# Hybrid decoder step on one core: a turn's first score block is copied out of PSUM before the last gate function and the table load of the turn before

## The chip, the cores and the metric

The kernel runs on one core of a Trainium2 chip. The metric is the device time of one execution in microseconds (us). A core has TensorE (PE; its weight loads are listed as PEld), VectorE (DVE), ScalarE (ACT), GpSimd (POOL) and SyncE (SP, here the only issuer of DMAs). Each engine works through its own instruction stream in order; the streams meet at semaphores.

## The reference, cut to what matters

One inference step of a one-layer decoder, for a prompt of 16 + 1024 positions and 8 running sequences with one new token each. Stick-breaking attention and an RG-LRU branch run beside each other, are merged by sigmoid gates, and a ConvFFN follows.

```python
z = jnp.einsum('bqhgd,bshd->bhgqs', qb, kp) * SB_SCALE + bias_f
log_keep = jnp.where(mask, jax.nn.log_sigmoid(-z), 0.0)      # softplus of z
w = jnp.where(mask, jnp.exp(jax.nn.log_sigmoid(z) + tail), 0.0)   # tail: sum of later log_keep
...
r = sigmoid(xb @ w_rgate + b_rgate); i = sigmoid(xb @ w_igate + b_igate)
a = jnp.exp(-RG_C * r * softplus(-lam))
u = jnp.sqrt(-jnp.expm1(2.0 * log_a)) * i * xc
h = scan(a, u); rnn = h * gelu(gr)
x = x + (gate_a * attn + gate_b * rnn) @ w_out
```

The kernel writes softplus(z) as max(z, 0) + ln(1 + exp(-|z|)), every sigmoid by a tanh, and the square root through exp and ln. So ScalarE needs two table sets in turn: one with the gelu and tanh, one with exp and ln.

## The kernel before, in words

Five phases follow each other: the first projections, the mixing phase (here from about 200 to 1090 us), the output projection, the FFN and the last norm. The change lies in the mixing phase (`phase_mix`).

The mixing phase has 8 turns (`i` from 0 to 7), one for each pair of heads and for one tile of 128 RNN channels; the loop is unrolled. A turn has 17 slots (`s`), one for each block of 64 queries, in the order of `BLOCK_ORDER`. All four engines have their order written out by hand, and each slot has work from several pipeline stages:

- TensorE, slot s: values of the block of slot s-4 (L1355), transposes of the weights of slot s-3 (L1336), a few pieces of the RNN and gate projections (L87), in slots 2 to 9 the decode scores (L1395, they need ScalarE's copy `k_t`) and in slots 1 to 8 transposes of a K page (L1407), then the scores of slot s+1 (L1315, the mask at L1322). Only in slot 0 are the scores of slot 0 made as well, last but one: after the page products of the turn before (L1378). The scores of slot s+1 wait for `z_copied` of slot s, since there is one PSUM tile for scores (`p_z`).
- ScalarE, slot s: `score_out` copies the scores out of PSUM twice, as |z + bias| (L1029) and as z + bias (L1030, this one gives `z_copied`); in slots 2 to 9 the copy `k_t` (L1067); the exponential of the weights of slot s-2 (L1054); the high part of the next projection tile (`high_part`, L1002, in slot 1 among others); softplus by an exp (L1084) and a ln (L1085); the projection chunks out of PSUM (L1049); and one part of the RNN tail of the turn before (`act_late`: an exp in slot 0, a ln in slot 1, a ln in slot 2, an exp in slot 5).
- VectorE, slot s: values out (L1137), max(z, 0) of slot s-1 (L1144), its running sum, which needs softplus (L1151), copies of the transposed weights (L1129), z minus the sum (L1157), in slot 1 among others the low part of the projection tile, which needs the high part (L1117), and parts of the RNN tail; the one in slot 1 (L728) gives the stage on which `act_late` waits in the same slot.

At the head of slot 0 of every turn but the first, ScalarE works off the gate functions of the turn before: a load of the gelu and tanh set, a gelu, four tanh (together `act_gates`, all at L678 by the helper `act_step`), a sixth function that waits for VectorE's `gated` (L711), and `act.preload_act_table_set` (L692), which loads the exp and ln set. All of them come ahead of `score_out` of slot 0.

Turns 2, 4 and 6 begin with a new group of K and V heads: SP loads K anew, and the scores of slot 0 wait for it. Turns 1, 3, 5 and 7 keep K. In all of them, TensorE waits at the end of the turn before for the last V pages (L1378).

Of the kernel before, what the change touches and what calls it, by code (L numbers as in the profile page):

```python
# [20 lines left out]
KT = D // P  # L21
# [32 lines left out]
def nth(turn, per_turn, index, credit=0):  # L54

    return turn * per_turn + (index + 1 + credit)
# [599 lines left out]
class Branch:  # L656
# [23 lines left out]
    def act_gates(self, act, i):  # L680

        _, ga = self.views(i)
        gr, gb, rg, ig, rc = self.gr, self.gb, self.rg, self.ig, self.rc
        self.act_step(act, i, gr[:, :], gr[:, :], ACT.Gelu_apprx_tanh)
        self.act_step(act, i, gb[:, :], gb[:, :], ACT.Tanh, scale=0.5)
        self.act_step(act, i, rg[:, :], rg[:, :], ACT.Tanh, bias=rc[:, 2:3], scale=0.5)
        self.act_step(act, i, ga, ga, ACT.Tanh, scale=0.5)
        self.act_step(act, i, ig[:, :], ig[:, :], ACT.Tanh, bias=rc[:, 3:4], scale=0.5)
        act.wait_ge(self.gated, nth(i, 1, 0))

        self.act_step(act, i, gr[:, :], rg[:, :], ACT.Tanh, T_R, bias=rc[:, 1:2], scale=rc[:, 1:2])
        act.preload_act_table_set("natural_log_exp_and_others")  # L692

# [107 lines left out]
def phase_mix(nc, g, branch, first_tiles, sem):  # L801
# [3 lines left out]
    with ctx:  # L805
# [79 lines left out]
        with nc.Block() as block:  # L885
# [108 lines left out]
            @block.scalar  # L994
            def _(act):
                own = Chain(act, act_step)
                act.sem_inc(proj_out, 2)

                def high_part(slot, chunks, turns):
                    act.wait_ge(w_in[slot], turns)  # L1000
                    act.wait_ge(proj_done, chunks)
                    act.activation(w_hi[:, slot, :, :], w_raw[:, slot, :, :], ACT.Copy).then_inc(w_hi_ready, 1)  # L1002

                act.wait_ge(inits, 2)
                for h in range(2):
                    rows = slice(HD * h, HD * (h + 1))
                    act.activation(never[rows, :], z[rows, QB * h:QB * (h + 1)], ACT.Copy).then_inc(masks, 1)
                act.activation(ident_b[:, :], g.ident[:, :], ACT.Copy).then_inc(masks, 1)
                act.sem_inc(z_copied, 1)
                high_part(0, CHUNK_NS, 16)  # L1010
                act.preload_act_table_set("natural_log_exp_and_others")

                def score_out(i, s, first):

                    b, q0, nq, nk = unit(s)
                    so, zs, pz = sums[:, soft_cols(s)], z[:, z_cols(s)], p_z[:, 0:min(nk, 1024)]
                    act.wait_ge(qk_done, nth(i, SLOTS, s, SLOTS))
                    if not first or s >= 2:
                        act.wait_ge(arg_ready, nth(i, SLOTS, s - 2, 1))
                    if not first or s > LAG:  # L1020
                        act.wait_ge(wt_turned, nth(i, GROUPS, group_of(s - LAG, 0) - 1, GROUPS))
                    if b == 16:
                        act.activation(so[:, 1024:nk], p_z_last, ACT.Abs, bias=bias[:, 0:1])
                        act.activation(zs[:, 1024:nk], p_z_last, ACT.Identity, bias=bias[:, 0:1])
                        so, zs = so[:, 0:1024], zs[:, 0:1024]
                    elif b >= 2:
                        pz = p_z[:, 0:1024].rearrange("p (a c) -> p a c", a=2)[:, :, 0:nk // 2]
                        so, zs = (x.rearrange("p (a c) -> p a c", a=2) for x in (so, zs))
                    own.mark(act.activation(so, pz, ACT.Abs, bias=bias[:, 0:1]))  # L1029
                    act.activation(zs, pz, ACT.Identity, bias=bias[:, 0:1]).then_inc(z_copied, 1)  # L1030

                def chunk_out(i, n, first):

                    what, c = CHUNK_ORDER[n]
                    cols = slice(CW * c, CW * (c + 1))
                    if what == "ga":
                        out = g.mix[:, bass.ds(i + 1, 1), cols].rearrange("p a c -> p (a c)")
                    else:
                        out = {"xr": xr, "gr": gr, "gb": gb, "rg": rg, "ig": ig}[what][:, cols]
                    if n == 0 and not first:  # L1040
                        act.wait_ge(xc_ready, nth(i, 1, 0) - 1)
                    if what in ("gr", "rg", "gb") and c == 0 and not first:
                        done = {"gr": S_ROOT, "rg": S_STATE}
                        if what in done:
                            act.wait_ge(branch.stage, nth(i - 1, STAGES, done[what]))
                        else:
                            act.wait_ge(branch.tail_done, nth(i, 1, 0) - 1)
                    act.wait_ge(proj_done, nth(i, CHUNK_NS, n, CHUNK_NS))
                    act.activation(out, p_proj[:, CHUNK_BANK[n], 0:CW], ACT.Copy).then_inc(proj_out, 1)  # L1049

                def weights(i, s):

                    act.wait_ge(arg_ready, nth(i, SLOTS, s, 1))
                    act.activation(z[:, z_cols(s)], z[:, z_cols(s)], ACT.Exp).then_inc(w_ready, 1)  # L1054

                def slots(i, first):
                    own.turn(0, i, 2 * SLOTS + 3)
                    own.step(act.activation(bias[:, 0:1], g.bias_pair[:, bass.ds(i, 1)], ACT.Copy))
                    for s in range(SLOTS):
                        if s == 0 and not first:  # L1060
                            weights(i, -2)
                            act.wait_ge(proj_out, nth(i, CHUNK_NS, -1, 2))
                            branch.act_gates(act, i - 1)
                        score_out(i, s, first)
                        if 2 <= s <= 9:
                            act.wait_ge(page_used, nth(i, 16, s - 2, 2))
                            act.activation(k_t[:, :, :].rearrange("p a c -> p (a c)"), p_kt[:, :],  # L1067
                                           ACT.Copy).then_inc(kt_out, 1)
                        if s >= 2 or s == 1 and not first:
                            weights(i, s - 2)  # L1070
                        if s in W_AT:
                            t = W_AT.index(s)
                            high_part((t + 1) % 2, nth(i, CHUNK_NS, CHUNK_NS - 1) if t == 0
                                      else nth(i, CHUNK_NS, TILE_LAST[t - 1], CHUNK_NS), 16 * (nth(i, 2, (0, 1, 1, 2)[t])))
                        if s == 11:
                            act.wait_ge(zd_read, nth(i, 1, 0))
                            own.step(act.activation(softd[:, :, :], zd[:, :, :], ACT.Abs))
                            own.step(act.activation(softd[:, :, :], softd[:, :, :], ACT.Exp, scale=-1.0))
                            act.activation(softd[:, :, :], softd[:, :, :], ACT.Ln, bias=1.0).then_inc(softd_done, 1)
                        for n in EARLY_OUT.get(s, ()):  # L1080
                            chunk_out(i, n, first)
                        so = sums[:, soft_cols(s)]
                        act.wait_ge(act_step, own.base + own.n)
                        own.step(act.activation(so, so, ACT.Exp, scale=-1.0))  # L1084
                        act.activation(so, so, ACT.Ln, bias=1.0).then_inc(soft_done, 1)  # L1085
                        for n in chunks_of(s):
                            if n not in EARLY_OUT.get(s, ()):
                                chunk_out(i, n, first)
                        if not first and s in ACT_LATE_AT:
                            branch.act_late(act, i - 1, ACT_LATE_AT[s])  # L1090
                        if s == 13:
                            act.wait_ge(argd_ready, nth(i, 1, 0))
                            act.activation(zd[:, :, :], zd[:, :, :], ACT.Exp).then_inc(wd_ready, 1)
                    assert own.n == 2 * SLOTS + 3

                for i in range(KT):
                    slots(i, i == 0)
                weights(KT, -2)
                weights(KT, -1)
                act.wait_ge(proj_out, nth(KT, CHUNK_NS, -1, 2))  # L1100
                branch.act_gates(act, KT - 1)

            @block.vector
            def _(dve):
# [1122 lines left out]
```

## Time and profile before

| | |
|---|---|
| median of 3 runs | 2044.91 us (2043.24 to 2045.83) |
| profiled execution | 2048.54 us, span of its records 2046.8 us |
| TensorE granted clock, mean | 0.965 of 2.4 GHz |
| TensorE busy | 1893.0 us, 92% of the span |
| VectorE busy | 1210.6 us, 59% |
| ScalarE busy | 928.8 us, 45% |
| one turn of the mixing phase, from one load of the gelu set to the next | 109 to 112 us |

The span runs from the first to the last recorded instruction; the execution has 1.7 us around it. A busy share is an average over five phases with different limits. For this change the stretch of some 20 us at the head of a turn is what is to be read, seven times: turn 1 begins near 300 us, turn 7 near 964 us.

### The profile page before, as it was taken

To read this page: it belongs to the slowest core of one execution; us is meant where nothing else is said; L and a number is where in the kernel's file an instruction comes from. 1 tells how busy PE (TensorE), PEld (TensorE's weight loads), DVE (VectorE), ACT (ScalarE), POOL (GpSimd) and SP (SyncE) were. 2 spreads that over 40 slices of the span, in tenths; PEclk is the share of its full clock that TensorE was granted. 3 is DMA by queue.
4 is the path that set the end of the run, shared out by engine and by line. 5 is a ranking of instruction groups with operands and counts; after the bars stand their busy time and mean duration, and the time that the engine had idled before them with its cause. 6 is when DMAs were issued, how large, how long until landed. Compare 5 with 4: busy or idle time off the path is not lost. (4 is left out here: it accounts for less than half of the span.)

```text
span 2046.8 us, 38456 instructions
## 1 busy us (share of the span) xinstructions
PE 1893.0 (92%) x14580; PEld 1730.1 (85%) x14580; DVE 1210.6 (59%) x1999; ACT 928.8 (45%) x1506; POOL 199.2 (10%) x98
## 2 busy tenths in 40 slices
PE   6998999989998999899996978999999999999985
PEld 5897878878787878687884768999999999999984
DVE  6101667768685858577776435665566556656655
ACT  5121677776867686777775221221222122212213
POOL 0121000000000000000000002221122112211210
PEclk9999999989998999999997989999999999999988
DMA  4334213141314232331313321111111111111104
GB/s 134 109 89 111 79 46 97 44 109 40 99 48 103 63 79 68 82 85 43 98 36 100 123 73 42 58 52 41 41 51 51 41 41 51 51 37 45 51 11 182
DMA packets 198685, 143.47 MB, mean 70 GB/s; under 512 B 58289, under 2 KB 187890, under 8 KB 198528
## 3 DMA queue, kind: packets, MB, share of 16 engines
q1 hardware_dynamic: 198554, 141.73, 24.4%
q8 instruction: 82, 1.34, 0.3%
q14 instruction: 49, 0.40, 0.1%
HBM read 124.31 MB, written 17.61 MB: 69 GB/s over the span
## 5 line engine op out<-in xcount | busy, mean ns | idle before, releaser
L87 PE MATMUL d_p_up<-n_hi,d_w_hi 128*128 128x346 f32 x1056 | 342.2, 324 | 16.3 <-ACT d_up L1824 8.3
L87 PE MATMUL d_p_up<-n_hi,d_w_lo 128*128 128x346 f32 x1056 | 341.4, 323 | 0.0
L87 PE MATMUL d_p_up<-n_lo,d_w_hi 128*128 128x346 f32 x1056 | 341.3, 323 | 0.0
L1927 DVE TENSOR_TENSOR mix<-mix,d_p_down 128x346 f32<-128x346 f32 x264 | 136.1, 515 | 268.2 <-PE d_p_down L1976 268.2
L87 PE MATMUL b_p_proj<-n_hi,b_w_hi 128*128 128x350 f32 x768 | 264.9, 345 | 16.0 <-DVE b_w_lo L1117 9.4
L1779 POOL TENSOR_TENSOR d_w_lo<-w_raw,d_w_hi 128x1024 fp32r<-128x1024 f32 x45 | 109.0, 2424 | 1468.6 <-ACT d_w_hi L1810 1468.6
L87 PE MATMUL b_p_proj<-n_lo,b_w_hi 128*128 128x350 f32 x768 | 251.7, 328 | 0.0
L87 PE MATMUL b_p_proj<-n_hi,b_w_lo 128*128 128x350 f32 x768 | 251.4, 327 | 0.0
L1824 ACT ACTIVATE d_up<-d_p_up 128x346 f32<-128x346 f32 x132 | 60.1, 457 | 401.8 <-PE d_p_up L87 401.8
L87 PEld LDWEIGHTS d_p_up<-n_hi,d_w_hi 128*128 128x128 f32 x1056 | 200.6, 190 | 17.4 <-ACT d_up L1824 9.1
L87 PEld LDWEIGHTS d_p_up<-n_lo,d_w_hi 128*128 128x128 f32 x1056 | 201.0, 190 | 0.0
L87 PEld LDWEIGHTS d_p_up<-n_hi,d_w_lo 128*128 128x128 f32 x1056 | 200.7, 190 | 0.0
L1151 DVE TENSOR_TENSOR_SCAN b_sums<-b_sums 128x720 f32<-128x720 f32 (+16 forms) x136 | 171.1, 1258 | 8.0 <-ACT b_sums L1085 3.4
L87 PEld LDWEIGHTS b_p_proj<-n_hi,b_w_hi 128*128 128x128 f32 x768 | 149.5, 195 | 18.4 <-issue 10.1
L1976 PE MATMUL d_p_down<-d_a_lo,d_wd_hi 128*128 128x346 f32 x480 | 153.8, 320 | 0.0
L1976 PE MATMUL d_p_down<-d_a_hi,d_wd_hi 128*128 128x346 f32 x480 | 153.8, 320 | 0.0
L1976 PE MATMUL d_p_down<-d_a_hi,d_wd_lo 128*128 128x346 f32 x480 | 153.7, 320 | 0.0
L1137 DVE COPY mix<-b_p_misc 128x64 f32<-128x64 f32 (+1 forms) x136 | 29.7, 219 | 205.6 <-PE b_p_misc L1355 205.3
L87 PEld LDWEIGHTS b_p_proj<-n_lo,b_w_hi 128*128 128x128 f32 x768 | 149.2, 194 | 0.0
L87 PEld LDWEIGHTS b_p_proj<-n_hi,b_w_lo 128*128 128x128 f32 x768 | 148.1, 193 | 0.0
L1029 ACT ACTIVATE b_sums<-b_p_z,b_bias 128x720 f32<-128x720 f32 (+16 forms) x136 | 94.8, 697 | 109.9 <-PE b_p_z L1322 97.6
L1315 PE MATMUL b_p_z<-b_k_in,b_q_in 64*64 64x360 f32 (+16 forms) x1024 | 96.5, 438 | 20.4 <-issue 20.4
(262 smaller groups left out, 3837.8 us busy)
## 6 DMA issues: line engine op xcount, KB each, us to landing
w_raw<-in_w_in SPq DMA_DIRECT2D x45, 512.0 KB, 4.6
w_raw<-in_w_up SPq DMA_DIRECT2D x45, 512.0 KB, 3.9
b_page<-in_cache_k SPq DMA_DIRECT2D x128, 128.0 KB, 2.1
b_page<-in_cache_v SPq DMA_DIRECT2D x128, 128.0 KB, 2.1
w_raw<-in_w_down SPq DMA_DIRECT2D x22, 512.0 KB, 3.5
b_q_in<-q_scr SPq DMA_DIRECT2D x272, 32.0 KB, 2.2
mix<-in_x_prompt SPq DMA_DIRECT2D x8, 512.0 KB, 7.1
w_raw<-in_w_out SPq DMA_DIRECT2D x8, 512.0 KB, 3.5
```

Of the source, the lines that this page charges most:

```text
L87: last = pe.matmul(out, w[:, k, :], x[:, k, col:col + width], start=(k == 0 and w is w_hi and x is x_hi), stop=(k == KT - 1 and w is w_lo))
L1029: own.mark(act.activation(so, pz, ACT.Abs, bias=bias[:, 0:1]))
L1137: dve.tensor_copy(g.mix[:, bass.ds(i if s >= 0 else i - 1, 1), FIRST + q0:FIRST + q0 + nq] .rearrange("p a c -> p (a c)"), p_av[:, 0:nq]). ...
L1151: dve.tensor_tensor_scan(pos[:, ::-1], so[:, ::-1], pos[:, ::-1], 0.0, ALU.add, ALU.add)\
L1315: last = pe.matmul(banks[bank][QB * a:QB * (a + 1), 0:k1 - k0], q_in[rows, Q_AT[s], a, :], k_in[rows, k0:k1], start=True, stop=k1 <= diagonal)
L1779: pool.tensor_tensor(w_lo[:, slot, :, :], w_raw[:, raw, :, :], w_hi[:, slot, :, :].bitcast(F32), ALU.subtract).then_inc(lo_ready, 1)
L1824: act.activation(up[:, u % 2, F0 + FW * c:F0 + FW * (c + 1)], p_up[:, n % 2, 0:FW], ACT.Copy).then_inc(up_out, 1)
L1927: dve.tensor_tensor(to, to, p_down[:, n % 4, 0:FW], ALU.add).then_inc(down_out, 1)
L1976: last = pe.matmul(p_down[:, n % 4, 0:FW], w[:, k, P * tile:P * (tile + 1)], a[:, k, F0 + FW * c:F0 + FW * (c + 1)], start=(k == 0 and w i ...
```

## The change

The sixth gate function and the table load leave `act_gates` and become a method of their own. In turns 1 to 7, ScalarE now runs them behind `score_out` of slot 0 instead of ahead of it. At the end of the phase, where no scores follow, both methods are called one after the other. No instruction is added or removed, no semaphore and no buffer is changed.

```diff
@@ class Branch
         self.act_step(act, i, ig[:, :], ig[:, :], ACT.Tanh, bias=rc[:, 3:4], scale=0.5)
+
+    def act_last_gate(self, act, i):
+
+        gr, rg, rc = self.gr, self.rg, self.rc
         act.wait_ge(self.gated, nth(i, 1, 0))
-
         self.act_step(act, i, gr[:, :], rg[:, :], ACT.Tanh, T_R, bias=rc[:, 1:2], scale=rc[:, 1:2])
         act.preload_act_table_set("natural_log_exp_and_others")
@@ phase_mix, ScalarE, slots(i, first)
                             branch.act_gates(act, i - 1)
                         score_out(i, s, first)
+                        if s == 0 and not first:
+                            branch.act_last_gate(act, i - 1)
                         if 2 <= s <= 9:
@@ phase_mix, ScalarE, after the last turn
                 branch.act_gates(act, KT - 1)
+                branch.act_last_gate(act, KT - 1)
```

## Rows read from the trace of the kernel before

**Rows 1.** The page, busy time and share of the span by engine.

```profile
PE 1893.0 (92%) x14580; PEld 1730.1 (85%) x14580; DVE 1210.6 (59%) x1999; ACT 928.8 (45%) x1506; POOL 199.2 (10%) x98
```

**Rows 2.** Timeline, ScalarE, head of turn 1 (start us, us, instruction, idle before).

```profile
300.52 1.28 ACT L678 ACT_TABLE_LOAD   x1
301.82 1.08 ACT L678 ACTIVATE r_gr<-r_gr 128x1050 f32<-128x1050 f32 x1
...
306.86 1.25 ACT L678 ACTIVATE r_gr<-r_rg,r_rc 128x1050 f32<-128x1050 f32 x1
308.13 1.28 ACT L692 ACT_TABLE_LOAD   x1
309.43 0.86 ACT L1029 ACTIVATE b_sums<-b_p_z,b_bias 128x720 f32<-128x720 f32 x1
310.18 0.85 ACT L1030 ACTIVATE b_z<-b_p_z,b_bias 128x720 f32<-128x720 f32 x1
310.93 0.80 ACT L1084 ACTIVATE b_sums<-b_sums 128x720 f32<-128x720 f32 x1
311.76 0.80 ACT L1085 ACTIVATE b_sums<-b_sums 128x720 f32<-128x720 f32 x1
```

**Rows 3.** Timeline, TensorE, turn 1: scores of slots 0 and 1.

```profile
308.13 0.20 PE L1322 MATMUL b_p_z<-b_never,b_ident_b 64*64 64x64 bf16 x2
311.14 0.37 PE L1315 MATMUL b_p_z<-b_k_in,b_q_in 64*64 64x168 f32 x4 [2.81 <-issue]
```

**Rows 4.** Timeline, TensorE, scores of slot 1 in turns 3, 5 and 7.

```profile
531.62 0.84 PE L1315 MATMUL b_p_z<-b_k_in,b_q_in 64*64 64x168 f32 x8 [3.17 <-issue]
...
753.38 0.84 PE L1315 MATMUL b_p_z<-b_k_in,b_q_in 64*64 64x168 f32 x8 [3.42 <-issue]
...
975.12 0.84 PE L1315 MATMUL b_p_z<-b_k_in,b_q_in 64*64 64x168 f32 x8 [3.91 <-issue]
```

**Rows 5.** Timeline, VectorE and ScalarE, slots 1 and 2 of turn 1.

```profile
314.06 1.66 DVE L1151 TENSOR_TENSOR_SCAN b_sums<-b_sums 128x720 f32<-128x720 f32 x1
...
314.90 1.05 ACT L1002 ACTIVATE b_w_hi<-w_raw 128x1024 fp32r<-128x1024 f32 x1
...
317.36 1.22 DVE L1117 TENSOR_TENSOR b_w_lo<-w_raw,b_w_hi 128x1024 fp32r<-128x1024 f32 x1
...
319.98 1.17 ACT L678 ACTIVATE r_xc<-r_gr,r_rc 128x1048 f32<-128x1048 f32 x1 [2.79 <-DVE r_ig L728]
...
322.65 0.59 ACT L1067 ACTIVATE b_k_t<-b_p_kt 128x512 f32<-128x512 f32 x1
```

**Rows 6.** Timeline, TensorE weight loads, turn 1, slot 2: decode scores.

```profile
323.36 0.97 PEld L1395 LDWEIGHTS b_p_misc<-q_block,b_k_t 128*128 128x128 f32 x8 [0.41 <-issue]
```

**Rows 7.** Timeline, head of turn 2: ScalarE, VectorE, TensorE weight loads.

```profile
420.49 0.86 ACT L1029 ACTIVATE b_sums<-b_p_z,b_bias 128x720 f32<-128x720 f32 x1 [2.15 <-PE b_p_z L1322]
...
425.96 1.04 ACT L1002 ACTIVATE b_w_hi<-w_raw 128x1024 fp32r<-128x1024 f32 x1
...
428.63 1.22 DVE L1117 TENSOR_TENSOR b_w_lo<-w_raw,b_w_hi 128x1024 fp32r<-128x1024 f32 x1
...
433.93 0.59 ACT L1067 ACTIVATE b_k_t<-b_p_kt 128x512 f32<-128x512 f32 x1
...
434.82 1.02 PEld L1395 LDWEIGHTS b_p_misc<-q_block,b_k_t 128*128 128x128 f32 x8
```

**Rows 8.** Timeline, turn 6, slot 2: ScalarE's copy and TensorE's decode scores.

```profile
876.72 0.60 ACT L1067 ACTIVATE b_k_t<-b_p_kt 128x512 f32<-128x512 f32 x1
...
878.04 1.02 PEld L1395 LDWEIGHTS b_p_misc<-q_block,b_k_t 128*128 128x128 f32 x8
```

**Rows 9.** Windows, TensorE, turn 3 (length, busy, matmuls, granted clock, DMA share, GB/s).

```profile
531.62:536.60 4.98, 4.98 (x39) 0.50 0.76 205
```

**Rows 10.** Windows, the projection's matmuls (L87) alone, turn 3, columns as before.

```profile
535.00:536.50 1.50, 1.50 (x6) 0.50 0.17 35
537.00:538.50 1.50, 1.50 (x11) 1.00 0.16 29
```

## Prediction

> **What bounds the kernel now.** I read the page first. TensorE is busy 92% of the span, ScalarE 45% [rows 1]: over the whole step TensorE is the bound, and a change of ScalarE's order can only give what TensorE loses by waiting for it. So I then read the timelines of the seven turn heads, engine by engine, then the decode scores further on in each head, since that is where TensorE next needs something that ScalarE makes late in its order, and last the granted clock.
>
> The reader is to see three things. In turn 1 TensorE ends the scores of slot 0 at 308.33 and starts those of slot 1 at 311.14, 2.81 us idle [rows 3]. The page calls it "issue", but the wait is `z_copied`: ScalarE runs the sixth gate from 306.86, the table load from 308.13, and only then the two copies, whose second ends at 311.03 [rows 2], 0.11 ahead of TensorE's start. Second, in turns 2, 4 and 6 it isn't so: there ScalarE has done gate and load and waits for the scores, 2.15 us in turn 2 [rows 7]. Third, two slots on, TensorE's first decode scores need `k_t`. In turn 1 ScalarE ends that copy at 323.24 [rows 5] and TensorE, idle 0.41, goes on at 323.36 [rows 6], 0.12 later: it waits there. The chain to that copy doesn't start with TensorE: ScalarE's ln ahead of it waits 2.79 us for VectorE's L728 [rows 5], and VectorE works up to there in its order from the running sum at 314.06, which needs the softplus that ended at 312.56 [rows 2, 5].
>
> **The change part by part.** Nothing is added or removed; two instructions are moved behind two others.
>
> *What is gained at slot 1.* ScalarE can start the copies 0.04 after the scores (turn 2: the wait ends when the scores land). From that start TensorE's next scores follow in 1.71 (309.43 to 311.14). So a non-fresh turn needs 1.75 from the end of its scores, and gains its idle time less that: 2.81 - 1.75 = 1.06 in turn 1 [rows 3]; 3.17, 3.42 and 3.91 less 1.75 give 1.42, 1.67 and 2.16 in turns 3, 5 and 7 [rows 4]. That is 6.31 us. In turns 2, 4 and 6 the scores come late either way, and nothing is gained. The 0.04 is an estimate; between 0.0 and 0.12 (the handover of [rows 5, 6]) the sum moves by 0.3.
>
> *What is put back.* Gate and load took 306.86 to 309.43, 2.57 us [rows 2]. All that ScalarE does behind the copies comes 2.57 later, less what the copies come earlier: 2.57 - 1.06 = 1.51 in turn 1, then 1.15, 0.90 and 0.41 in turns 3, 5 and 7, and the full 2.57 in turns 2, 4 and 6. Behind them stand, in order, the exp and ln of slot 0, the tail's exp, the copies of slot 1, an exponential of weights, the high part, softplus of slot 1, a projection chunk and the ln that waits for VectorE. The new wait of the first copy for the scores is in these numbers.
>
> *Where the delay lands.* On VectorE in slot 1: the running sum waits for softplus, and behind it stand the copies of transposed weights, z minus sum, the low part, L728. In turn 1 the sum had 314.06 - 312.56 = 1.50 of room, the low part behind the high part (ending at 315.95) 317.36 - 315.95 = 1.41 [rows 5], so the low part gives way first: VectorE comes 1.51 - 1.41 = 0.10 late. In turn 2 that room is 428.63 - 427.00 = 1.63 [rows 7]; I take it for the other five as well. Fresh turns: 2.57 - 1.63 = 0.94 late. Turns 3, 5, 7: 1.15, 0.90 and 0.41 less 1.63, that is 0.48, 0.73 and 1.22 early (VectorE's other input, TensorE's values, comes early by more). ScalarE's ln follows VectorE, and the `k_t` copy follows that ln, so `k_t` moves by the same amounts.
>
> *What TensorE makes of it.* At the decode scores it can't go on before `k_t` plus 0.12. In turn 1 it stood at that limit: the 1.06 is lost, and 0.10 more. In turn 2 it came 434.82 - 434.52 = 0.30 behind the copy [rows 7], 0.18 over the limit; in turn 6 878.04 - 877.32 = 0.72 [rows 8], 0.60 over. I take 0.18 for turns 3, 4, 5 and 7. So turns 3, 5 and 7 gain 0.48 + 0.18 = 0.66, 0.91 and 1.40, together 2.97; turn 1 loses 0.10; turns 2 and 4 lose 0.94 - 0.18 = 0.76 each and turn 6 0.94 - 0.60 = 0.34, together 1.86.
>
> *What I count at nothing.* TensorE's scores of slot 2 need the copies of slot 1, late by the same 0.4 to 2.6; the transposes and projection pieces of slot 1 cover that. VectorE's weight copies, up to 0.94 late in fresh turns, have the same cover ahead of the values of slot 2. Were the cover gone, the 0.94 would come at slot 2 in place of the decode scores, 0.2 to 0.6 more a fresh turn. SP's loads wait on TensorE's scores and page products and move with them; no DMA is among the moved instructions. Past the decode scores all engines are shifted alike, and TensorE carries its shift to the next turn's head. At the end of the phase the order is unchanged.
>
> *Sum.* -2.97 + 0.10 + 1.86 = -1.0 us: the span goes from 2046.8 to 2045.8, the profiled execution from 2048.5 to 2047.5. It stands 3.6 over the median of the runs shown, so the forecast is 2044.91 - 1.0 = 2043.9 us. What can be told from no change is some 0.2%, 4.1 us.
>
> *The price of the load behind the copies.* A load is followed by the next function 1.30 after its start, also where that function needs the table at once (300.52 to 301.82, and 308.13 to 309.43) [rows 2]; that is in the 2.57. The Trainium skill, ScalarE: Activation LUTs, "What ACT_TABLE_LOAD costs", gives a drain of 1380 ns on top of a 1283 ns load for each switch; the rows show the 1.28 and no such drain. By the page, each of the seven delays would be 1.36 larger, and the sum about +8.5 us instead of -1.0.
>
> **The rivals.**
>
> *The slot-1 gain stays* (faster). If `k_t` had slack that I don't see, the four turns would keep 6.3 us, less 1.9 for the fresh turns: 2040.5, or 2038.6 without that loss. Against it: TensorE goes on 0.12 to 0.72 behind the copy in the three turns shown [rows 5 to 8], so hardly 0.6 of an early arrival can be kept.
>
> *The clock falls in the new wait* (slower). TensorE now idles at the decode scores instead of at slot 1: what it gains at slot 1 beyond `k_t`, 1.2 in turn 1 and about 0.8 in turns 3, 5 and 7, more where it runs at the full clock sooner. In turn 3, after the idle 3.17 [rows 4], it worked 4.98 us at half the clock (0.50 of 2.4 GHz, that is 1.2) [rows 9], and in 1.50 us it started 6 projection matmuls there and 11 at the full clock [rows 10]. So one such stretch costs 4.98 x (1 - 6/11) = 2.3 us, behind the decode scores all of it on TensorE's path. One or two give +1.3 or +3.6, still no change that can be told; from three on it is slower, +5.9, and four give +8.2, 2053. For it: the clock fell at turn heads where TensorE was idle. Against it: the new idle time is shorter than those, and stands between dense projection work.
>
> *The full delay reaches TensorE in the fresh turns* (slower). If VectorE's room in turns 4 and 6 were none, they and turn 2 would pay 2.57 each: -2.97 + 0.10 + 7.71 = +4.8, 2049.7. Turn 2's 1.63 speaks against it.
>
> *The table load costs more in its new place* (slower). The exp now stands right behind it, and if the two cost one load's 1.30 more there, each delay is 1.30 larger: turns 1 to 7 cost 1.40, 2.06, 0.64, 2.06, 0.39, 1.64 and 0 us, 8.2 in all, 2053.1. Both places in [rows 2] speak against it; in the first the gelu that needs the table stands right behind the load. The page named above is the one by which this would happen. The same size comes out if the copies of slot 0 can't run under the gelu set and a load is put ahead of them, and one behind: a change that doesn't do what it says. The Trainium skill, ScalarE: Activation LUTs, "Table sets: the hidden batching unit", has abs and identity in every set; no row here shows either under the gelu set.
>
> **How the numbers follow.** My forecast 0.60; the clock falls in one or two turns 0.18, in three or four 0.08; the slot-1 gain stays 0.06; the full delay in fresh turns 0.04; dearer or added loads 0.04. That is faster 0.06, same 0.78, slower 0.16. The predicted time is the likeliest case, 2043.9. Its own range is 2042.0 to 2045.9: 1.9 lower if the fresh turns' loss is hidden, 2.0 higher if the gains of turns 3, 5 and 7 are mostly lost. The range takes in one or two falls of the clock, up to 2043.9 + 4.6 = 2048.5, and downward the runs' own spread of a us: 2041.0 to 2048.6, with 0.78 inside.
>
> **What would show it.** Right: in turns 1, 3, 5 and 7 the idle time ahead of the slot-1 scores shrinks to 1.75; in all seven the running sum or the low part waits for ScalarE; ScalarE's wait for L728 shrinks; and TensorE has a new idle time ahead of the first decode scores, ended by the `k_t` copy, the gap from copy to weight load being 0.12. Turns 2, 4 and 6 become longer by under 1 us. Wrong: decode scores that start over 1 us earlier in turns 1 and 3; a granted clock of 0.50 behind the decode scores; a table load between L678 and L1029; or gaps over 1.3 between a load and the function behind it.

## The result, and the profile after

The changed kernel took 2052.8 us (median of 6 runs, 2049.8 to 2054.2), the kernel before 2045.4 us beside it (6 runs, 2043.2 to 2048.5): a ratio of 1.0026, with a 95% interval of 1.0016 to 1.0036. It is slower by 0.26%, and the interval leaves out no change, where no change was forecast and 2048.6 was the top of the range. The profiled execution took 2051.28 us with a span of 2049.5.

The head of turn 1 went as the prediction drew it. ScalarE's timeline, to be set beside [rows 2]:

```profile
304.29 1.16 ACT L678 ACTIVATE r_ig<-r_ig,r_rc 128x1050 f32<-128x1050 f32 x1
306.54 0.86 ACT L1032 ACTIVATE b_sums<-b_p_z,b_bias 128x720 f32<-128x720 f32 x1 [1.10 <-PE b_p_z L1328]
307.30 0.85 ACT L1033 ACTIVATE b_z<-b_p_z,b_bias 128x720 f32<-128x720 f32 x1
308.04 1.26 ACT L678 ACTIVATE r_gr<-r_rg,r_rc 128x1050 f32<-128x1050 f32 x1
309.32 1.28 ACT L695 ACT_TABLE_LOAD   x1
310.62 0.80 ACT L1089 ACTIVATE b_sums<-b_sums 128x720 f32<-128x720 f32 x1
```

TensorE's timeline there, beside [rows 3]: the scores of slot 1 wait 1.77 us instead of 2.81.

```profile
306.29 0.20 PE L1328 MATMUL b_p_z<-b_never,b_ident_b 64*64 64x64 bf16 x2
308.25 0.84 PE L1321 MATMUL b_p_z<-b_k_in,b_q_in 64*64 64x168 f32 x8 [1.77 <-issue]
```

No load stands between the gates and the copies, and the exp follows its load after 1.30. VectorE's running sum now waits for softplus in all seven turns, 1.00 to 1.35 us; in turn 2:

```profile
424.76 1.66 DVE L1157 TENSOR_TENSOR_SCAN b_sums<-b_sums 128x720 f32<-128x720 f32 x1 [1.01 <-ACT b_sums L1090]
```

The wait that was to come at the decode scores is there as well. The copy and TensorE's weight loads (L1401 is L1395 of before) in turn 7, timelines of the two engines:

```profile
983.80 0.19 PEld L87 LDWEIGHTS b_p_proj<-n_hi,b_w_lo 128*128 128x128 f32 x1
...
984.90 0.59 ACT L1072 ACTIVATE b_k_t<-b_p_kt 128x512 f32<-128x512 f32 x1
...
985.60 1.21 PEld L1401 LDWEIGHTS b_p_misc<-q_block,b_k_t 128*128 128x128 f32 x8 [1.62 <-issue]
```

In the kernel before, the same copy and weight loads of turn 7, without idle time ahead of the loads:

```profile
986.85 0.59 ACT L1067 ACTIVATE b_k_t<-b_p_kt 128x512 f32<-128x512 f32 x1
...
987.75 1.02 PEld L1395 LDWEIGHTS b_p_misc<-q_block,b_k_t 128*128 128x128 f32 x8
```

A granted clock of 0.50 behind the decode scores was among the prediction's signs of being wrong, and it is there. It shows in windows of TensorE (columns as in [rows 9]): after the wait the clock falls to half. First the changed kernel in turn 7, the wait and 6.8 us behind it:

```profile
983.99:985.60 1.61, 0.29 (x2) 1.00 0.59 170
985.60:992.40 6.80, 6.76 (x49) 0.55 0.24 60
```

Then the kernel before, the same 6.8 us of the same turn:

```profile
987.75:994.55 6.80, 6.80 (x78) 1.00 0.21 52
```

The reader is to see 49 matmuls where there were 78. From its decode scores to the next load of the gelu set that turn took 92.22 us against 89.35, as the lengths of these windows tell, first after, then before:

```profile
985.60:1077.82 92.22, 89.08 (x879) 0.96 0.21 55
```

```profile
987.75:1077.10 89.35, 86.26 (x881) 1.00 0.21 56
```

So this one fall (a stretch at half clock behind the decode scores) cost 2.87 us, against the 2.3 of the prediction's rival.

### The profile page after: what moved, and what is told of

Its sections match the earlier page's. It is cut to its first block and busy times, and to the rows that moved or that the text cites. A ratio compares the mean times of both kernels' runs of the same rounds, so it can differ in the third digit from the quotient of the medians.

```text
span 2049.5 us, 38456 instructions
## 1 busy us (share of the span) xinstructions
PE 1898.2 (93%) x14580; PEld 1733.1 (85%) x14580; DVE 1210.9 (59%) x1999; ACT 929.4 (45%) x1506; POOL 199.2 (10%) x98
## 5 line engine op out<-in xcount | busy, mean ns | idle before, releaser
L87 PE MATMUL d_p_up<-n_hi,d_w_hi 128*128 128x346 f32 x1056 | 342.2, 324 | 16.2 <-ACT d_up L1830 8.3
L87 PE MATMUL d_p_up<-n_hi,d_w_lo 128*128 128x346 f32 x1056 | 341.4, 323 | 0.0
L87 PE MATMUL d_p_up<-n_lo,d_w_hi 128*128 128x346 f32 x1056 | 341.2, 323 | 0.0
L87 PE MATMUL b_p_proj<-n_hi,b_w_hi 128*128 128x350 f32 x768 | 264.8, 345 | 16.0 <-DVE b_w_lo L1123 9.4
L87 PE MATMUL b_p_proj<-n_lo,b_w_hi 128*128 128x350 f32 x768 | 251.7, 328 | 0.0
L87 PE MATMUL b_p_proj<-n_hi,b_w_lo 128*128 128x350 f32 x768 | 251.3, 327 | 0.0
L87 PEld LDWEIGHTS d_p_up<-n_hi,d_w_hi 128*128 128x128 f32 x1056 | 200.6, 190 | 17.5 <-ACT d_up L1830 9.2
L87 PEld LDWEIGHTS d_p_up<-n_lo,d_w_hi 128*128 128x128 f32 x1056 | 201.1, 190 | 0.0
L87 PEld LDWEIGHTS d_p_up<-n_hi,d_w_lo 128*128 128x128 f32 x1056 | 200.7, 190 | 0.0
L87 PEld LDWEIGHTS b_p_proj<-n_hi,b_w_hi 128*128 128x128 f32 x768 | 149.6, 195 | 18.4 <-issue 10.1
L87 PEld LDWEIGHTS b_p_proj<-n_lo,b_w_hi 128*128 128x128 f32 x768 | 149.0, 194 | 0.0
L87 PEld LDWEIGHTS b_p_proj<-n_hi,b_w_lo 128*128 128x128 f32 x768 | 148.1, 193 | 0.0
L1135 DVE COPY b_w_t<-b_p_wt 128x512 f32<-128x512 f32 (+5 forms) x216 | 110.4, 539 | 3.9 <-PE b_p_wt L1342 3.6
```

The source lines that it names most:

```text
L87: last = pe.matmul(out, w[:, k, :], x[:, k, col:col + width], start=(k == 0 and w is w_hi and x is x_hi), stop=(k == KT - 1 and w is w_lo))
L1135: dve.tensor_copy(w_t[0:rows, W_T_AT[q % GROUPS], 0:here, :], p_wt[0:rows, p_wt_at(q), 0:here, :]).then_inc(wt_out, 1)
```

## The experiments

Two theories stood against each other. The clock theory: TensorE's new wait at the decode scores lets the clock fall behind it, and that is the loss. The rival: ScalarE and VectorE stay late past slot 2, and turns grow later on, at the full clock. Ratios are to the kernel before, with 95% intervals; 23 to 25 runs of it stood beside each set. A profile shows one execution of a run.

**again, again_2, again_3**: the changed kernel, unaltered.

> The changed kernel once more, unaltered, for a second profile and more times. Both theories expect the time of the changed kernel, some 7 us (0.3%) over the kernel before. The clock theory (after the new waits at the decode scores of slot 2 the granted clock falls, at random among the turns) expects a stretch at 0.50 behind the decode scores again, in one to three turns, each costing 2 to 3 us, and not in the same turns as in the first profile (only turn 7). The rival (the lateness of ScalarE and VectorE lives on past slot 2 and shows as waits later in the turn) expects turns that are longer between the decode scores and the next load of the gelu set than the 86.1 us of the kernel before, at the full clock.

> The changed kernel, a third profile, to count falls. The clock theory expects one to three stretches at 0.50 behind the decode scores of turns 1, 3, 5 and 7, none in turns 2, 4 and 6, and turns 1 to 7 together longer by 1.5 us for a short and 3 us for a long stretch than the head's terms alone make them.

> The changed kernel, a fourth profile, with the same expectation as again_2.

Measured: 2052.6 us (6 runs), 1.0027 (1.0013 to 1.0040); the two single runs 2051.5 and 2053.0. Windows of the profile of again, turn 1, then turn 7: the wait, full clock, half clock, and in turn 1 full clock again and the whole way to the next turn.

```profile
321.72:323.95 2.23, 0.29 (x2) 1.00 0.47 133
323.95:326.10 2.15, 2.12 (x30) 1.00 0.07 15
326.10:329.50 3.40, 3.40 (x27) 0.50 0.38 96
329.50:332.00 2.50, 2.50 (x22) 1.00 0.02 7
...
323.95:411.55 87.60, 86.10 (x869) 0.98 0.22 57
...
989.14:990.70 1.56, 0.29 (x2) 1.00 0.53 168
990.70:991.60 0.90, 0.87 (x8) 1.00 0.33 58
991.60:998.40 6.80, 6.80 (x47) 0.51 0.21 54
```

From its decode scores to the next load of the gelu set, the fifth of these windows, turn 1 took 87.60 us, where the kernel before took 86.09 at the full clock:

```profile
323.36:409.45 86.09, 84.59 (x869) 1.00 0.23 59
```

Again_2 and then again_3 show the same two falls, in turn 1 and turn 7:

```profile
325.10:328.50 3.40, 3.40 (x34) 0.51 0.35 96
...
990.50:997.30 6.80, 6.80 (x47) 0.51 0.20 52
```

```profile
323.20:326.60 3.40, 3.40 (x34) 0.53 0.32 89
...
989.10:996.00 6.90, 6.90 (x46) 0.51 0.22 51
```

So a fall came in turn 7 in four executions of four, in turn 1 in three, and in no other turn. That it would not stay with the same turns was a miss, and so was a price of 2 to 3 us for each, since those in turn 1 cost 1.5. That turns without a fall don't grow was not: turns 2, 4 and 5 took 86.1 to 86.2 us from the decode scores on in all four, as before, turn 6 took 86.4 to 86.7 (before 86.4 and 86.5), and turn 3, with 87.1 and 87.2 before, took 86.1 to 87.1. That speaks against the rival. Why turn 3 varies is not shown.

The length of a wait doesn't settle alone whether a fall follows. The four profiles have 15 waits of 1.5 us or more at the decode scores: the seven in turns 1 and 7 were followed by a fall, the eight in other turns were not. Why is open.

How long the wait is goes with the clock earlier in the same turn. In the changed kernel the decode scores start at a fixed time behind the scores of slot 0 (15.2 us, see the account below), so the less of that time TensorE runs at half clock, the earlier it is there and the longer it waits. The half clock at the head of turn 7, first before, then after, with the way from there to the wait:

```profile
973.60:980.40 6.80, 5.28 (x40) 0.50 0.72 197
```

```profile
972.60:976.00 3.40, 3.40 (x32) 0.50 1.12 310
976.00:983.99 7.99, 7.99 (x76) 1.00 0.24 58
```

In turns 1, 3, 5 and 7 of the four profiles, 6.8 or 10.2 us at half clock at the head went with 0.2 to 0.6 us of wait at the decode scores, 3.4 us with 1.5 to 1.7, and none (turn 1 of again) with 2.2.

**before_again**: the kernel before, unaltered.

> The kernel before once more, for a second profile. The clock theory expects falls of the granted clock at the heads of the turns, before the scores of slot 1, as in the first profile, and none behind the decode scores of slot 2; the turn lengths agree with those of the first profile within a microsecond.

Measured: 2045.7 us. Falls at the turns' heads, none behind the decode scores. Turn 6 was 1.05 us shorter than in the first profile, the other turns agree within 0.4; turns 1 to 7 together took 776.06 us against 776.58.

**odd_turns, even_turns**: the change in some turns alone.

```diff
                             branch.act_gates(act, i - 1)
+                            if not (i % 2 == 1):        # even_turns: i % 2 == 0
+                                branch.act_last_gate(act, i - 1)
                         score_out(i, s, first)
-                        if s == 0 and not first:
+                        if s == 0 and not first and i % 2 == 1:
                             branch.act_last_gate(act, i - 1)
```

> The change in turns 1, 3, 5 and 7 alone, where K is kept; turns 2, 4 and 6 as before. By the terms of the prediction: 2.5 to 2.9 us less than the kernel before, if the clock doesn't fall. The clock theory expects the falls here, since the new wait at the decode scores is 1 to 1.6 us long in these turns: a gain eaten up or turned into a loss, 0 to 6 us slower than the kernel before. The rival that the loss is in turns 2, 4 and 6 expects 2.5 to 3 us faster.

> The change in turns 2, 4 and 6 alone, where the scores of slot 0 come late and gate and load stood in their shadow. By the terms of the prediction: 1.9 us slower than the kernel before. The clock theory expects that and no more, 1 to 3 us, since the new waits there are 0.2 to 0.8 us. The rival that these turns carry the whole loss expects 6 to 8 us slower.

Measured: odd_turns 2048.1 us (12 runs, 2042.8 to 2051.6), 1.0001 (0.9993 to 1.0010); even_turns 2048.1 (11 runs), 1.0008 (0.9999 to 1.0017). Odd_turns has falls behind the decode scores of turns 1, 3 and 5, and none in turn 7:

```profile
325.55:328.95 3.40, 3.40 (x34) 0.56 0.35 93
547.60:551.00 3.40, 3.40 (x35) 0.53 0.33 87
769.70:773.10 3.40, 3.40 (x31) 0.50 0.40 96
988.80:995.60 6.80, 6.78 (x78) 1.00 0.25 60
```

Those three turns took 87.6 us from the decode scores on, where the kernel before took 86.1, 87.1 and 86.2. The 2.5 to 2.9 us that were to be gained are gone: in this profile the ways from the scores of slot 0 to the decode scores came out 2.9 to 3.6 us shorter than before (103.3 us over the seven turns, see the table below), and the ways from there to the next load 3.1 us longer (610.7). Even_turns shows no fall, though its waits in turns 2, 4 and 6 were 1.0 to 1.1 us, longer than expected. Its loss is 1.6 us by the ratio, with an interval of -0.2 to 3.5: that takes in the term (1.9 us) and nothing at all, and leaves out 6 to 8. The parts add up to less than the whole, +1.8 us against +5.5; with these intervals, and other turns falling, that is not to be resolved.

**keep_busy, keep_busy_more**: the wait filled.

```diff
                         j = s - 2
+                        if s == 2 and i % 2 == 1:
+                            for _ in range(12):     # keep_busy_more: 24 if i == 7 else 14
+                                pe.matmul(p_misc[:, 144:256], w_hi[:, 0, 0, :], g.n_hi[:, 0, 0:112],
+                                          start=True, stop=True)
                         pe.wait_ge(kt_out, nth(i, 8, j))
```

> The change, and in turns 1, 3, 5 and 7 twelve added matmuls of 112 columns on TensorE ahead of its wait for the copy at the decode scores; their result is never read. They fill about a microsecond of that wait and do nothing else. The clock theory expects no stretch at 0.50 behind the decode scores of these turns, and the changed kernel's time less what the falls cost: 2046 to 2048, at or just under the kernel before. The rival (lateness that lives on, not the clock) expects the time of the changed kernel, 2052 to 2053, or some more, for TensorE has more to do.

> As keep_busy, with 14 added matmuls in turns 1, 3 and 5 and 24 in turn 7, where 12 had left half of the wait open and the clock still fell (a matmul of them took 0.11 us). The clock theory expects no stretch at 0.50 behind the decode scores in any turn, and, with up to 0.7 us overshoot a turn, 2046 to 2048: at the kernel before within 1.5 us, some 5 under the changed kernel. If the falls are not what costs, the time is that of the changed kernel or over it, 2052 to 2055.

Measured: keep_busy 2049.1 us (12 runs), 1.0018 (1.0009 to 1.0027). That is over the 2046 to 2048 expected, and the interval meets that of the changed kernel. In its profile, taken of the fastest of the twelve, turns 1, 3 and 5 have no fall, but turn 7 has. There the twelve filled 1.47 us and 0.71 us of wait was left:

```profile
983.54 1.47 PEld L1400 LDWEIGHTS b_p_misc<-n_hi,b_w_hi 128*128 128x128 f32 x12
985.72 0.63 PEld L1405 LDWEIGHTS b_p_misc<-q_block,b_k_t 128*128 128x128 f32 x5 [0.71 <-ACT b_k_t L1072]
```

Keep_busy_more, 2050.5 us (12 runs), 1.0016 (1.0007 to 1.0025), has no fall in any of the four turns of its profile:

```profile
322.90:329.70 6.80, 6.80 (x80) 1.00 0.19 52
547.05:553.85 6.80, 6.80 (x80) 1.00 0.17 48
769.90:776.70 6.80, 6.80 (x80) 1.00 0.21 53
991.95:998.75 6.80, 6.80 (x80) 1.00 0.18 49
```

From decode scores to next load its seven turns sum to 608.2 us, near the kernel before (607.6) and not the changed kernel (611.2, below), though single turns without a fall were up to 1.0 us off either way. Its time came down by 2 us where 5 were expected, and its interval meets that of the changed kernel. The filling overshot, by 1.2 us in turn 3 and 1.5 in turn 7, 3.4 over all seven. So the profiles show no fall behind a wait that was filled altogether, and a way past the decode scores of about the old length; the times alone show neither.

**ln_later, before_ln_later, odd_ln_later**: the wait taken away at its source. The copy `k_t` stood behind the tail's first ln, and that behind VectorE's L728; now the ln comes after the copy.

```diff
-ACT_LATE_AT = {0: 0, 1: 1, 2: 2, 5: 3}
+ACT_LATE_AT = {0: 0, 2: 1, 3: 2, 5: 3}
```

> The change, and the tail's first ln moved from slot 1 to the end of slot 2, behind ScalarE's copy for the decode scores (the second ln goes from slot 2 to slot 3). That copy no longer waits for VectorE's late chain. The clock theory expects no wait at the decode scores, no fall of the clock behind them, and all that was gained at slot 1: about 5 us less than the kernel before, near 2040. The rival, lateness that lives on past slot 2, expects at most what the waits at the decode scores were worth, some 4 us less than the changed kernel, still 2 to 4 us over the kernel before.

> The kernel before, with the tail's first ln moved behind the copy for the decode scores as in ln_later, gate and load left ahead of the scores. If the gain of ln_later came from the change's gain at slot 1, kept because the copy no longer waits for VectorE, this run gains next to nothing: 0 to 1 us, the 0.4 that TensorE waited in turn 1. If moving the ln is the gain by itself, it is 8 to 10 us faster, near 2038.

> ln_later with the change in turns 1, 3, 5 and 7 alone. If the change costs turns 2, 4 and 6 something even without the wait at the decode scores, this is 1 to 2 us faster than ln_later, 2036 to 2037; if their cost was that wait alone, the two are equal within a microsecond. Both theories expect it 8 to 11 us under the kernel before.

Measured: ln_later 2038.0 us (5 runs), 0.9952 (0.9939 to 0.9964); before_ln_later 2046.0 (12 runs), 0.9997 (0.9989 to 1.0006); odd_ln_later 2041.1 (7 runs), 0.9968 (0.9956 to 0.9980). In the profile of ln_later TensorE goes from projection to decode scores without a wait in every turn, though the profiled execution was the slowest of the five (2042.8 us); turn 7, ScalarE and TensorE:

```profile
980.03 0.61 ACT L1072 ACTIVATE b_k_t<-b_p_kt 128x512 f32<-128x512 f32 x1
...
981.61 0.19 PEld L87 LDWEIGHTS b_p_proj<-n_hi,b_w_lo 128*128 128x128 f32 x1
981.77 1.02 PEld L1401 LDWEIGHTS b_p_misc<-q_block,b_k_t 128*128 128x128 f32 x8
...
983.21 1.16 ACT L678 ACTIVATE r_xc<-r_gr,r_rc 128x1048 f32<-128x1048 f32 x1
```

and the clock holds behind them:

```profile
981.77:988.57 6.80, 6.80 (x78) 1.00 0.35 95
```

Neither move gains by itself, the two together gain some 9 us, where about 5 were expected. In this profile the ways from the scores of slot 0 to the decode scores sum to 98.8 us, 7.5 less than in the changed kernel, whose waits at the decode scores summed to 4.8 to 10.3 us in its four profiles, 8.1 in the mean. Odd_ln_later was slower than ln_later where equal or faster was expected, and some 6 us under the kernel before where 8 to 11 were expected. Its intervals meet those of ln_later, and its profile has the shorter turns; whether the change pays in turns 2, 4 and 6 once the copy is free stays open.

**pieces_moved**: real work in place of the wait.

```diff
-        count = 6 if s < 8 or s % 3 == 0 else 5
+        count = {2: 9, 3: 3}.get(s, 6 if s < 8 or s % 3 == 0 else 5)
```

> The change, and three of the six projection pieces of slot 3 (nine matmuls, 1.45 us) moved to slot 2, ahead of the decode scores: real work in place of the wait. Both the wait and the falls go: the clock theory with the terms of the prediction expects 5 to 9 us less than the kernel before, near ln_later (2038 to 2042). If lateness of ScalarE and VectorE past slot 2 is what costs, the wait only moves to slot 3, and the time stays within 2 us of the changed kernel.

Measured: 2040.5 us (11 runs), 0.9971 (0.9962 to 0.9980), as the clock theory expected. No fall behind the decode scores, and at most 0.44 us of wait there (turn 7). The wait didn't move to slot 3, where the rival had it. The ways from the scores of slot 0 to the decode scores sum to 108.9 us here; less the moved work, 7 x 1.45 us, that is 98.7, as in ln_later.

## Why the prediction was wrong

The sum of turns 1 to 7, from the gelu load of turn 1 to that behind turn 7, in us, as read from the start and end times of the timelines: from load to the end of the scores of slot 0, from there to the decode scores, and from there to the next load.

```
                        to scores   to decode   to next load   sum
before                    62.16      106.86       607.56      776.58
before_again              62.27      106.24       607.55      776.06
after                     63.00      106.24       609.57      778.81
again                     63.82      106.24       611.66      781.72
again_2                   62.95      106.38       611.61      780.94
again_3                   63.82      106.36       611.81      781.99
mean after - before       +1.2       -0.2         +3.6        +4.5
```

- **The gain at slot 1** was right: idle 1.75 to 1.77 us in every changed turn, where 1.75 was worked out.
- **The delay, and where it lands**, were right: in the changed kernel the decode scores start 15.17 to 15.21 us behind the scores of slot 0 in all 28 turns of four profiles. The prediction's terms, added to the 14.37 to 16.54 of its own trace, put them at 15.03 to 15.20. The whole head follows ScalarE's order through VectorE to the copy. ScalarE's wait for VectorE's L728 shrank from 2.8 to 3.0 us to 1.4. One link was another: the running sum waits for ScalarE in all 28 turns (1.0 to 1.8 us), and the low part, which was to give way first, in none. In the first pair of profiles the head's sum is -0.6, over all six -0.2, since the second profile of the kernel before took 0.6 less there; -1.0 was forecast.
- **The load's price** was right: 309.32 to 310.62 is 1.30. The drain that the Trainium skill, ScalarE: Activation LUTs, "What ACT_TABLE_LOAD costs", adds to a load does not show behind this one either. The copies (abs and identity in the kernel) ran under the gelu set without a load of their own. That agrees with the Trainium skill, ScalarE: Activation LUTs, "Table sets: the hidden batching unit", which has both in every set.
- **The step that failed** is the forecast's choice to leave the clock out: "the clock falls in the new wait" was a rival, at 0.26 in all, and the forecast's 0.60 counted the wait as TensorE's time alone. The rival took the new wait for about 0.8 us in turn 7; it was 1.53 to 1.62 in all four profiles. Falls came in turns 1 and 7, one in the first profile and two in each of the three others, worth 2.8 to 3.5 us in turn 7 (92.1 to 92.8 against 89.3) and 1.5 in turn 1. In the mean of the four they make +4.1, and turn 3, which came out 0.5 shorter, leaves the +3.6. The rival's price, 2.3, lay between the two. The argument against it, that the new idle time is shorter than that at the heads and stands between dense projection work, fell with the first profile.
- **Also mis-set** was the range. Its top took in two falls on top of the head's -1.0 and nothing else, and the head gave -0.2. The scores of slot 0 end +1.2 us later over the seven turns. They follow the last V pages, and single turns spread by up to 1.2 us between executions of one kernel, so that this is the change's doing is not shown. Outside the turns the six spans leave 1267.9 to 1270.7 us, 0.6 more after the change in the mean, within that spread. These 1.2 and 0.6 stay open; with the 4.5 they make the 5.1 by which the spans differ, and the runs' medians differ by 5.5 to 7.4.

That the falls, and not lateness, are what the time past the decode scores grew by is shown by the turns of the four profiles: without a fall none is longer than before by more than 0.3 us, and turn 1 took 86.1 us without one and 87.6 with one. That the wait at `k_t` is the cause of both losses, the gain of slot 1 and the falls, is shown by ln_later and pieces_moved, which take it away by different means and turn the loss into a gain of 0.3 to 0.5%.

## What to carry to other kernels

When a wait is moved from one place to another on the engine that bounds the kernel, ask what its clock does behind the new place: here a wait of 1.5 to 2.2 us in front of dense matmuls cost 1.5 to 3.5 us beyond its own length in turns 1 and 7, where the clock fell behind it. A gain ahead of a second wait is worth little until that wait is taken away too, so follow the engine's own next need (here `k_t`, and through it ScalarE's order and VectorE's chain) and change both in one go. A change that loses alone can be half of one that wins.

## What the runs showed of the hardware

A wait of 1.5 to 2.2 us, between stretches in which TensorE was busy throughout, was followed by a stretch at half clock in some executions and turns and not in others (turn 7 of odd_turns waited 0.5 us and had none; turn 3 of again waited 1.6 us and had none; turn 3 of odd_turns waited 1.55 us and had one). Over the profiles of the changed kernel and odd_turns that was so behind 10 of 13 such waits in turns 1, 3, 5 and 7, and behind none of five in turns 2, 4 and 6. Half clock took the matmuls of 6.8 us from 78 to between 47 and 49. With twelve added matmuls and 0.71 us of wait left, the clock fell all the same.
